# Where the last quarter of a later step's gram and its first mask stand in the chunk steps of an RWKV-7 kernel

## What is computed

```
def step(S, inp):
    r_t, w_t, k_t, v_t, a_t, b_t = inp
    sa = jnp.einsum('bhvk,bhk->bhv', S, a_t)
    S = (S * w_t[:, :, None, :] + sa[..., None] * b_t[:, :, None, :]
         + v_t[..., None] * k_t[:, :, None, :])
    return S, jnp.einsum('bhvk,bhk->bhv', S, r_t)
```

## Time and profile before

| | us |
|---|---|
| median of three runs | 1822.23 |
| lowest, highest run | 1818.08, 1826.13 |
| profiled execution, its own time | 1819.75 |
| its span (first to last instruction) | 1818.0 |
| PE busy | 1692.6 (93%) |
| DVE busy | 1047.8 (58%) |
| ACT busy | 799.1 (44%) |
| POOL busy | 642.8 (35%) |

### The profile page before, as it was taken

One profiled execution on the slowest core, in us unless ns is written; L12 is line 12 of the kernel. 1 busy time (PEld: TensorE's weight loads), 2 busy tenths in 40 slices (PEclk: granted clock), 3 DMA queues, 4 the chain that ended last, 5 costly groups with the idle time before them and its releaser, 6 DMA issues. The chain is left out here.

```text
span 1818.0 us, 27211 instructions
## 1 busy us (share of the span) xinstructions
PE 1692.6 (93%) x11264; PEld 1343.7 (74%) x11264; DVE 1047.8 (58%) x1367; ACT 799.1 (44%) x1198; POOL 642.8 (35%) x352
## 2 busy tenths in 40 slices
PE   8998999999999899798999999989999999988883
PEld 6876777888888787687888888868888886544441
DVE  5247945566755415775647677443126627866675
ACT  3355433332223334633233222343347736866673
POOL 1348513424444333951333444434421021222210
PEclk8999999999999899999999999989999999999997
DMA  8224231225444333232223544333420066999994
GB/s 347 82 93 115 73 89 59 81 71 207 172 164 151 116 103 115 73 109 51 72 69 128 193 163 163 140 117 133 145 81 1 2 265 258 386 392 395 391 393 178
DMA packets 82610, 288.04 MB, mean 158 GB/s; under 512 B 30473, under 2 KB 30601, under 8 KB 65332
## 3 DMA queue, kind: packets, MB, share of 16 engines
q1 hardware_dynamic: 76708, 275.87, 42.1%
q0 software_dynamic: 5040, 8.25, 1.4%
q10 hardware_dynamic: 736, 2.14, 0.3%
HBM read 274.50 MB, written 22.61 MB: 163 GB/s over the span
## 5 line engine op out<-in xcount | busy, mean ns | idle before, releaser
L1585 POOL TENSOR_TENSOR wmem_r<-wmem,wmem_r 128x1024 fp32r<-128x1024 f32 x170 | 431.3, 2538 | 687.4 <-ACT wmem_r L1087 592.5
L744 PE MATMUL banks<-h_hi_r,wmem_r 128*128 128x512 f32 x1632 | 510.0, 391 | 5.7 <-POOL wmem_r L1585 3.6
L744 PEld LDWEIGHTS banks<-h_hi_r,wmem_r 128*128 128x128 f32 x1632 | 306.7, 188 | 73.6 <-issue 5.4
L1087 ACT ACTIVATE wmem_r<-wmem 128x1024 fp32r<-128x1024 f32 x170 | 180.2, 1061 | 408.9 <-DMA wmem<-wstream 405.6
L744 PE MATMUL banks<-hT_r,wmem_r 128*128 128x512 f32 x816 | 317.9, 390 | 0.0
L744 PEld LDWEIGHTS banks<-hT_r,wmem_r 128*128 128x128 f32 x816 | 153.4, 188 | 32.2 <-issue 0.8
L2793 DVE TENSOR_TENSOR slots_r<-slots,wmem_r 128x1024 fp32r<-128x1024 f32 x102 | 121.9, 1218 | 56.3 <-ACT wmem_r L2486 47.8
L2874 POOL TENSOR_TENSOR wmem_r<-wmem,wmem_r 128x1024 fp32r<-128x1024 f32 x30 | 74.7, 2491 | 201.2 <-ACT wmem_r L2344 201.2
L1525 DVE SCALAR_TENSOR_TENSOR ztp<-xT,c_act,ztp 128x256 f32<-128x256 f32 x168 | 124.9, 743 | 6.0
L1038 PE MATMUL banks<-slots_r,wmem_r 128*128 128x512 f32 x512 | 127.7, 389 | 0.0
L764 PE MATMUL banks<-wmem_r,h_hi_r 128*128 128x512 f32 x384 | 118.9, 391 | 0.0
(11 more groups left out here) (454 smaller groups left out, 3000.2 us busy)
## 6 DMA issues: line engine op xcount, KB each, us to landing
wmem<-wstream SPq DMA_DIRECT2D x206, 512.0 KB, 3.3
slots<-experts SPq DMA_DIRECT2D x80, 1024.0 KB
xT<-ada SPq DMA_DIRECT2D x24, 1024.0 KB, 5.5
xT<-experts SPq DMA_DIRECT2D x16, 1024.0 KB
slots<-ada SPq DMA_DIRECT2D x8, 1024.0 KB, 18.0
x_keep<-xT SPq DMA_DIRECT2D x2, 2048.0 KB
xT<-x_keep SPq DMA_DIRECT2D x2, 2048.0 KB
dil_rows<-dil_once SPq DMA_DIRECT2D x1, 2560.0 KB
```

The source lines that it names most:

```text
L744: mm = nc.tensor.matmul(o, r(lhs[:, k, :]), r(rhs[:, k, :]), start=(k == 0 and i == 0), stop=(k == KD - 1 and i == 2))
L1087: inc(nc.scalar.activation(r(chunk(b)[0]), w, ACT.Copy), "w_high")
L1585: inc(g.tensor_tensor(r(lo), lo, r(hi), ALU.subtract), "w_split")
```

## The change

On PE the whole gram of step m + 3 (c = 0 to 3) is issued behind w's state part and ahead of the wait for `w_ready0`; nothing of it is left between y's state part and s. On VectorE the mask of the gram's first bank stands ahead of the copy of u's first bank instead of behind it. `FULL` is reordered to match. The step has the same instructions, of the same sizes; no semaphore is added or removed.

```diff
@@ -417,7 +417,7 @@
         for m in range(STEPS):
             g = m + GRAMS_FIRST
-            names = [f"w{m}0", f"w{m}1", f"u{m}0", f"u{m}1"] + ([f"gram{g}0", f"gram{g}1"] if g < STEPS else [])
+            names = [f"w{m}0", f"w{m}1"] + ([f"gram{g}0", f"gram{g}1"] if g < STEPS else []) + [f"u{m}0", f"u{m}1"]
             names += ([f"s{m}"] if m < STEPS - 1 else []) + [f"y{m}0", f"y{m}1"]
@@ -935,7 +935,7 @@
                 if more:
                     o_g = gram_banks(m + GRAMS_FIRST)
-                    gram(m + GRAMS_FIRST, o_g, range(CW - 1))
+                    gram(m + GRAMS_FIRST, o_g, range(CW))
 
                 after("w_ready0", m + 1)
@@ -952,8 +952,6 @@
                 if m > 0:
                     state_part(o_y, R_, m, v_side, True, False)
-                if more:
-                    gram(m + GRAMS_FIRST, o_g, range(CW - 1, CW))
                 after("u_ready0", m + 1)
@@ -1408,9 +1406,9 @@
                 o = bank(f"u{m}0")[u_side(m, 0), 0:CW * RW_D].rearrange("p (c f) -> p c f", c=CW)
-                inc(v.tensor_copy(per_head(uv_of(m)[u_side(m, 0)])[:, 0], o), "u_ready0")
                 if m + GRAMS_FIRST < STEPS:
                     gram_mask(m + GRAMS_FIRST, 0)
+                inc(v.tensor_copy(per_head(uv_of(m)[u_side(m, 0)])[:, 0], o), "u_ready0")
                 if m < STEPS - 1:
```

## The result

The changed kernel takes 1830.71 us (median of 14 runs, 1826.01 to 1833.07) against 1822.65 us for the kernel before in the same comparison (14 runs). The ratio is 1.0039, its 95% interval 1.0029 to 1.0049: 5.3 to 8.9 us more. The sign was forecast, and it stays within the 0.5% that was called "same". But it is about three times the forecast 2.6 us, and above the range's upper end of 1829.6. The mechanism that the prediction gave is only part of it.

A forecast was written before the change was run, and what follows sets the result against it. PE bounds most of the kernel, a loop of dependent links the chunk steps. Step 0's 0.38, 2 x 0.28 and 2 x 0.18 make 1.30 us a layer, 2.6 in both; 1822.23 + 2.6 = 1824.8 us, range 1819.3 to 1829.6.

The forecast's parts named there:

- The step that failed: VectorE, steps 1 to 4: the first mask starts at S + 1.63, once the gram's bank is full, at best S + 1.18.
- S: Start of w's state part on PE in a chunk step; one period runs to the next, 4.19 or 4.29 us before.
- The rival that the change doesn't do what it says: PE ahead of u: the quarter gains nothing because w's copy ends last anyway; counted within the forecast, no chance of its own.
- The mask's hold: VectorE: the first mask holds the next instruction 0.61 us, so u's copy starts at S + 2.24, 0.28 us late.
- From u's copy to s: Chunk steps: s starts 0.57 us after u's copy starts, at S + 2.81.
- the forecast's periods: Steps 1 to 4: 4.47 us each, odd and even alike, +0.28 us for odd steps and +0.18 for even.
- u's own delay: PE ahead of u: the quarter's 0.21 us against 0.16 us of idle starts u at most 0.05 us later.
- Step 0: First chunk step of each layer, at the lower clock: u's copy starts at 256.32 instead of 255.94, +0.38 us.
- The forecast's other sum: Step 0: if u's 1.11 us from first record to copy stay whole, u is ready at 256.39, +0.45 us.
- The wake-up of PE ahead of s: Rival, chance 0.17: about 0.76 us of idle before s costs PE 0.15 us a step, 1.5 us more, 1826.3 us.
- The mask in the hole: Rival, chance 0.16 whole or in part: the mask starts by S + 1.35 and ends before u is ready, 1821.8 us.
- The clock: Rival, chance 0.03: longer holes bring PE's lower clock behind step 0, 2.0 us a step, 28 us in all, 1853 us.

The follow-up runs named there:

- both masks behind the scale: Kernel before with the first mask moved behind the state's scale, ahead of the second mask; PE as before: ratio 1.0029.
- the wait behind the mask: Changed kernel with the line that waits for u's bank moved below the first mask, directly ahead of u's copy: ratios 1.0028, 1.0022 and 1.0020 to the kernel before.
- the plain delay: Kernel before with an extra VectorE copy of u's first bank into unread memory ahead of its own copy, steps 0 to 4, both layers: ratios 1.0009 and 1.0016.
- PE's part alone: Changed kernel with u's copy ahead of the first mask again on VectorE: ratios 1.0012 and 1.0032 to the kernel before.
- VectorE's part alone: Kernel before with only VectorE's order changed (wait for u's bank, first mask, u's copy), the gram's last quarter left behind y's state part: ratio 1.0065.

## Why the prediction missed

**The step that failed** is the one that asks when the mask can start. It named two conditions, VectorE free at S + 1.18 and the gram's bank full at S + 1.13 plus 0.50, and left out the third: the wait for u's bank, which the diff shows as an unmoved line above the mask and which is an instruction of VectorE's queue like any other. With it the mask starts at u's readiness (S + 2.00 and 2.05 measured, not 1.63), and its whole hold falls on the loop. The rival that the change doesn't do what it says was set aside for PE's side and never asked of VectorE's. Had it been asked, the sum was at hand: S + 1.96 to 2.01 for u, 0.61 for the mask, 0.57 to s, 1.66 to S, 4.80 to 4.85 us a period against the 4.84, 4.88, 4.79 and 4.88 measured. In steps 1 to 4 the wait is worth 19.39 - 17.93 = 1.46 us in the first layer and 1.41 in the second, by the experiment that moves it.

**The mask's hold** was taken as 0.61 us from one pair of rows, for all steps. In the changed kernel u's copy starts 0.72 behind the mask in even steps (270.94 - 270.22) and 0.61 in odd ones. The rule of the Trainium skill that was weighed there (VectorE: DVE Perf Modes, Terms) gives 0.69. The even steps agree with it to 0.03, the odd ones do not, and the mask was mis-sized by 0.11 in half of the steps. What differs between them is the half of the partitions that the copy works on and the tile that it writes. The kernel with both masks behind the scale tells them apart: there w's copy writes the same tile in every step, and it too starts 0.71 us behind the mask where it works on partitions 64 to 127 (odd steps) and 0.60 behind it on 0 to 63. For u's copy the halves are the other way round. So the half counts, not the tile.

**From u's copy to s** was taken as 0.57. It is that only when ACT's copy ends with VectorE's, as in the kernel before. When VectorE's comes later, s follows in odd steps after 0.46 us: 3.12 - 2.66 in the changed kernel, 2.74 - 2.28 with the wait behind the mask, 2.77 - 2.31 with the plain delay (all from S); in even steps after 0.48 or 0.49 (3.21 - 2.72, 2.88 - 2.40, 2.78 - 2.30). So the first 0.1 us of a delay of VectorE's copy is free. This error cancels against the one of the mask's hold and against the mask's start at S + 1.67 instead of 1.63. It is by this luck, and not by right terms, that the kernel with the wait behind the mask took 17.93 us in steps 1 to 4, against the 17.88 of the forecast's periods; odd and even steps were not alike (4.41 and 4.55), as they should have been by the forecast.

**u's own delay** by the quarter was put at 0.05 us or less. The first load moved by 0.03 in odd steps (268.14 - 266.86 = 1.28 against 1.25) and not at all in even ones, but u's copy by 0.05 to 0.09 with the whole gram ahead. The loss of odd steps is what ate the gain of the even ones (4.28 against 4.19, 4.24 against 4.29).

**Step 0** was forecast at +0.38 us. It has the same fault: u is pushed back by the quarter and the mask comes on top. Over two profiles of each kernel it costs 1.5 us a layer, two fifths of the whole. The changed kernel's step 0 in its first profile:

```profile
256.48 1.84 PE L890 MATMUL banks<-slots 64*64 64x128 f32 x32 [0.75 <-issue]
...
259.21 0.69 DVE L1401 TENSOR_TENSOR gm_mem<-banks,cst 128x512 f32<-128x512 f32 x1 [3.00 <-PE banks L945]
259.94 0.43 DVE L1411 COPY rstd<-banks 64x256 f32<-64x256 f32 x1
```

u's copy starts 3.46 us behind the first gram record (259.94 - 256.48) against 2.45 (255.94 - 253.49), 1.0 us late. With PE's part alone it is 2.87 or 2.88 wherever the clock is low, so about 0.43 of this is the quarter ahead of u and about 0.6 the mask behind u's wait. The forecast's other sum, in which the 1.11 us stay whole (+0.45), was the right one for the quarter; the one that was taken left the mask's wait out here too. The rest goes with the lower clock, which held to the end of step 0 in the changed kernel's first layer (0.50 from 260 to 263 us) and had risen by then in the kernel before (1.00 from 257.00 to 258.17). This part is no fixed cost of a kernel: with PE's part alone, four step 0s took 5.22, 6.32, 3.95 and 6.32 us, two of them in one execution.

**The rivals.** The wake-up of PE ahead of s did not come: with 0.91 us of idle, s's first load in the changed kernel starts 0.06 us behind the end of the copy (271.43 against 270.94 + 0.43). So the 0.22 us ahead of u in step 5 has another cause, which was not looked for, and idle time was the wrong reading. The mask in the hole is refuted by S + 1.67. The clock did not fall again in the loop (in the changed kernel's second profile it is 1.00 from 265 us on in the first layer), as forecast, but it stretched step 0, which the prediction had treated as fixed, and it reached into step 1: 0.71 from 263.30 to 265.00, and a period of 5.22 us. That is a granted clock below 1.00 behind step 0, which the prediction had named as a sign of being wrong; it cost tenths of a microsecond and not the 2 us a step of the rival. The Trainium skill (TensorE: Matmul & The Clock Gate, on how oscillation bites in real kernels) warns of idle time between bursts. In step 0 of the changed kernel PE idles 1.45 us ahead of s and the clock stays low, which agrees; but it stayed at 0.50 through the second layer's step 0 of the kernel before as well, with 0.17 us idle there, so no run here shows that the idle time is the cause.

**The range** was built from the spread of the runs and the unknown costs of one mechanism; the case that would have held the result, a wait left in front of the mask, had no chance of its own. Its statement that both layers repeat the pattern of odd and even steps holds only roughly (4.68 us for step 4 of the second layer in the same profile).

**What stays open.** The kernel with the wait behind the mask lies 1.0020 to 1.0028 over the kernel before, some 4 us, where its chunk steps account for about 2. In its three profiles the stage ahead of the second layer's steps took 126.0, 126.2 and 124.8 us, against 120.8 and 122.6 in the kernel before, 123.3 and 122.9 in the changed one and 123.3 and 120.1 with a plain delay of nearly the same size. It was as long with VectorE's part alone (125.9) and with both masks behind the scale (125.7). The granted clock is lower there when it is long. This also bears on the comparison with the changed kernel: the chunk steps of the two differ by 5.9 us on average (76.3 and 70.4), their runs by some 3 us (an estimate from the ratios' averages, 1.0040 and 1.0023), and 2.6 us of the difference stand in this stage. What in a kernel brings the longer stage about, or whether it is chance, was not found.

## What to carry to other kernels

When a diff moves an instruction, read what the lines around it emit: a call that looks like an address may be a wait, and an instruction moved "ahead of a copy" is only ahead of the copy's wait if that line moves as well. Ask of each engine, not only of one, whether the change does what it says; the releaser in the profile's brackets answers it at once. On a loop of short dependent links, an instruction ahead of a link costs most of its length (the plain delay of 0.34 us cost 0.25 and 0.16, the mask of 0.69 held its follower for 0.61 or 0.72), and a plain dummy of known size measures how much of it is free.

## What was not expected of the hardware

- The distance from the mask to an independent next VectorE instruction took two values in one kernel, 0.61 and 0.72 us, for a mask of 0.69 us both times: the longer one where the next instruction works on partitions 64 to 127, with u's copy as with w's.
- An operation of 0.34 us put in front of one of two copies that a matmul waits for cost 0.25 us: both copies end together by the profile of the kernel before (260.55 on VectorE, 260.56 on ACT, below), yet there were 0.1 us to spare.

```profile
260.18 0.38 ACT L1204 ACTIVATE slots<-banks 64x256 f32<-64x256 f32 x1 [0.92 <-PE banks L945]
```

- A stage with the same instructions took between 120.1 and 126.2 us in the fourteen profiles taken of these kernels, by the granted clock. A difference of 2 us between two single profiles of this kernel says nothing unless it lies in the stage that was edited, and in step 0 not even then (3.95 to 6.32 us in one execution with PE's part alone).
